# Sixteen gate and up column pairs as seven block products each, their weight sums built in DRAM by adding transfers

## What is computed

```
h2 = rmsnorm(x, norm2_g)
x = x + (silu(h2 @ w_ffn_gate) * (h2 @ w_ffn_up)) @ w_ffn_down
```

## Time and profile before

| | |
|---|---|
| median of 3 runs | 3119.81 us |
| span of the profiled execution | 3118.1 us |
| what lies around the span, against the median | 1.7 us |
| PE busy | 3085.6 us, 99% |
| DVE busy | 1740.3 us, 56% |
| ACT busy | 1082.3 us, 35% |
| POOL busy | 311.3 us, 10% |
| moved by transfers | 536.49 MB, 172 GB/s mean |
| transfer queues | hardware 52.8% of 16 engines |

### The profile page before, as it was taken

How to read it: one execution, slowest core, us unless ns; L and a number is a source line. 1 busy time by engine, 2 the same in 40 slices (tenths; PEclk the granted TensorE clock), 3 DMA queues, 4 the chain that set the end, 5 groups by cost and what they waited for, 6 DMA issues and landing times.

```text
span 3118.1 us, 66114 instructions
## 1 busy us (share of the span) xinstructions
PE 3085.6 (99%) x27707; PEld 2627.9 (84%) x27707; DVE 1740.3 (56%) x2975; ACT 1082.3 (35%) x1979; POOL 311.3 (10%) x285
## 2 busy tenths in 40 slices
PE   8999999999999999999999999999999999999998
PEld 6877878888888788888888888998888889999998
DVE  6565645457776768355566375304666535554444
ACT  5544433344444444332233243303333312321112
POOL 0011110001111100000111000001111100022220
PEclk9999999999999999999999999999999999999999
DMA  5476566337666675344444473265444455466664
GB/s 183 161 245 203 164 197 188 96 102 250 206 219 208 221 261 198 95 149 143 143 149 143 146 255 95 89 215 184 135 130 130 135 162 171 151 226 197 196 202 138
DMA packets 272694, 536.49 MB, mean 172 GB/s; under 512 B 36240, under 2 KB 39696, under 8 KB 272400
## 3 DMA queue, kind: packets, MB, share of 16 engines
q1 hardware_dynamic: 272400, 532.27, 52.8%
HBM read 420.17 MB, written 112.08 MB: 171 GB/s over the span
## 4 chain that ended last, share of the span: by engine, by line
PE 96%; DVE 1%; ACT 1%; DMA 1%; issue 1%; SPq 0%; DVEq 0%; ACTq 0%
PE PS L1045 81%; PE PS L1109 6%; PE PS L1063 3%; PE PS L1168 1%; PE PS L1234 1%; PE PS L1408 1%; PE PS L1218 1%; PE PS L1158 1%; PE PS L1415 0%; PE PS L1194 0%; PE PS L1204 0%; PE PS L1102 0%; PE PS L1103 0%; DMA raw<-w 0%; PE PS L1069 0%
## 5 line engine op out<-in xcount | busy, mean ns | idle before, releaser
L1045 PE MATMUL PS<-hh,wh 128*128 128x512 f32 x1864 | 749.3, 402 | 0.2
L1045 PE MATMUL PS<-hh,wl 128*128 128x512 f32 x1864 | 727.5, 390 | 0.0
L1045 PE MATMUL PS<-hl,wh 128*128 128x512 f32 x1864 | 726.9, 390 | 0.0
L1452 ACT ACTIVATE wh<-raw 128x512 fp32r<-128x512 f32 x452 | 283.7, 630 | 418.7 <-PE PS L1045 349.3
L1957 DVE TENSOR_TENSOR wl<-raw,wh 128x512 fp32r<-128x512 f32 x452 | 321.0, 713 | 182.7 <-ACT wh L1452 179.6
L1045 PEld LDWEIGHTS PS<-hh,wh 128*128 128x128 f32 x1864 | 349.8, 188 | 80.7 <-issue 3.0
L1045 PEld LDWEIGHTS PS<-hh,wl 128*128 128x128 f32 x1864 | 349.8, 188 | 75.6
L1045 PEld LDWEIGHTS PS<-hl,wh 128*128 128x128 f32 x1864 | 350.4, 188 | 68.5 <-issue 1.0
L1045 PE MATMUL PS<-fh,wh 128*128 128x512 f32 x528 | 213.3, 404 | 0.0
L1045 PE MATMUL PS<-hh_last,wh 128*128 128x272 f32 x1024 | 212.8, 289 | 0.1
L1045 PE MATMUL PS<-hl_last,wh 128*128 128x272 f32 x1024 | 211.4, 288 | 0.0
(11 more groups left out here) (370 smaller groups left out, 5270.9 us busy)
## 6 DMA issues: line engine op xcount, KB each, us to landing
wh<-weight_hi SPq DMA_DIRECT2D x480, 256.0 KB, 2.7
wl<-weight_lo SPq DMA_DIRECT2D x480, 256.0 KB, 3.1
raw<-w SPq DMA_DIRECT2D x192, 512.0 KB, 3.8
weight_hi<-wh SPq DMA_DIRECT2D x164, 256.0 KB, 4.4
weight_lo<-wl SPq DMA_DIRECT2D x164, 256.0 KB, 4.6
raw<-w SPq DMA_DIRECT2D x96, 256.0 KB, 3.0
xres<-x SPq DMA_DIRECT2D x48, 256.0 KB, 4.7
gate_scratch<-gst SPq DMA_DIRECT2D x48, 256.0 KB, 3.6
```

The lines of the kernel that those rows point to most:

```text
L1045: mm = pe.matmul(PS[:, bank(t) + f, 0:t.cols], wt[:, cols], mov[:, m, (t.half + f) * t.cols:(t.half + f + 1) * t.cols], start=(first and a ...
L1452: act.activation(wh[h % 4][:], src, ACT.Copy).then_inc(hi_done, 1)
```

## The change

All four pairs of each of the last four groups (16 pairs in place of 8) become product pairs, and `SEVENS` has 16 members. The weight sums are no longer made by POOL in SBUF. They are built for all 16 pairs in a DRAM tensor `weight_sums` in the two stretches of stages B and W of one block and A of the next (16 transfers from the start of stage B of block 0 on, 16 from that of block 1 on, 16 quanta apart), by transfers that POOL issues: for each group eight transfers of 1 MiB from DRAM to DRAM, four that write (the first of sums 0 and 3, the copies of sum 0 to sum 1 and of sum 1 to sum 2) and four that add what they read to what is there (`accum_op`). Step (u, (row, half)) takes gate (row 0) or up (row 1) and that half into sum u. SP then loads four finished sums of 256 KB for each product pair into `sf`. Since the transfers only add, some signs change: the gate and up results come out negated, and four DVE additions become subtractions, the tanh's scale and a scalar change sign.

```diff
-SEVENS = [j for s in range(2, len(GROUPS)) for j in (sum(GROUPS[:s]), sum(GROUPS[:s]) + 1)]
+FIRST7 = 2
+SEVENS = [j for s in range(FIRST7, len(GROUPS)) for j in range(sum(GROUPS[:s]), sum(GROUPS[:s + 1]))]
...
-                    if j == 0:
-                        self.seven(b, s, sum(GROUPS[:s]))
+                    if j % 2 == 0:
+                        self.seven(b, s, sum(GROUPS[:s]) + j)
...
+    summed = nc.dram_tensor("weight_sums", (128, 4, len(SEVENS), WP), F32, kind="Internal").ap()
...
         def sum_tag(j, u):
             n = SEVENS.index(j)
-            return plan.first_of(SEVENS[n - n % 2]) - (58.0, 28.0)[n % 2] + 5.0 * u
+            if n % 4 < 2:
+                return plan.first_of(SEVENS[n - n % 2]) - (58.0, 28.0)[n % 2] + 5.0 * u
+            return plan.first_of(SEVENS[n - 2]) + 13.0 + 4.5 * u
...
+        SUM_STEPS = ((0, (1, 0)), (3, (0, 0)), (0, (1, 1)), (3, (1, 0)), (1, 0), (1, (0, 0)), (2, 1), (2, (0, 1)))
+
+        def sums_tag(i):
+            b, i = divmod(i, 4 * len(SUM_GROUPS))
+            return Q["B", b] + 6.0 + 16.0 * i
...
-            def halves_raw():
-                for j in SEVENS:
...
-                        sp.dma_start(raw[i][:], w[u]).then_inc(s_ld[i], 16)
+            def sums_in():
+                for n, j in enumerate(SEVENS):
+                    for u in range(4):
+                        yield max(sum_tag(j, u) - 9.0, sum_tag(SEVENS[n - 1], u) + 5.0 if n else -100.0)
+                        if n == 0:
+                            sp.wait_ge(dense, Q["late", 0])
+                            sp.wait_ge(s_made[u], 16 * 2 * len(SUM_GROUPS))
+                        else:
+                            sp.wait_ge(s_lo, 4 * (n - 1) + u + 1)
+                        sp.dma_start(sf[u][:], summed[:, u, n, :]).then_inc(s_ld[u], 16)
...
-                        act.wait_ge(s_f, made_sum(j, u))
+                        act.wait_ge(s_ld[u], 16 * (n + 1))
...
             def weight_sums():
-                a11, a12, a21 = raw[0][:, 0:WP], raw[0][:, WP:WU], raw[1][:, 0:WP]
...
-                        pool.tensor_tensor(sf[u][:], one, two, op).then_inc(s_f, 1)
+                for i, (s, (u, source)) in enumerate(itertools.product(SUM_GROUPS, SUM_STEPS)):
+                    yield sums_tag(i)
+                    n0, g = SEVENS.index(sum(GROUPS[:s])), GROUPS[s]
+                    out = summed[:, u, n0:n0 + g, :]
+                    done = 2 * SUM_GROUPS.index(s)
+                    if i % 8 >= 2 or s != SUM_GROUPS[0]:
+                        pool.wait_ge(s_made[u], 16 * (done + sum(1 for v, _ in SUM_STEPS[:i % 8] if v == u)))
+                    if isinstance(source, int):
+                        pool.wait_ge(s_made[source], 16 * (done + 2))
+                        pool.dma_start(out, summed[:, source, n0:n0 + g, :]).then_inc(s_made[u], 16)
+                        continue
...
+                    if any(v == u for v, _ in SUM_STEPS[:i % 8]):
+                        pool.dma_start(out, part, accum_op=ALU.add).then_inc(s_made[u], 16)
+                    else:
+                        pool.dma_start(out, part).then_inc(s_made[u], 16)
...
-                dve.tensor_tensor(u2[:], p0[:], psv(p3), ALU.add).then_inc(evac["V"], 1)
+                dve.tensor_tensor(u2[:], p0[:], psv(p3), ALU.subtract).then_inc(evac["V"], 1)
```

More of the change, by code:

```diff
@@ L637, in hybrid_layer @@
         t_f, t_hi, t_lo = sem("t_sum"), sem("t_hi"), sem("t_lo")
-        s_ld = [sem(f"s_raw{i}") for i in range(2)]
-        s_f, s_hi, s_lo, p_v, p_r = sem("s_sum"), sem("s_hi"), sem("s_lo"), sem("p_sum"), sem("p_scaled")
+        s_ld = [sem(f"s_ld{u}") for u in range(4)]
+        s_made = [sem(f"s_made{u}") for u in range(4)]
+        s_hi, s_lo, p_v, p_r = sem("s_hi"), sem("s_lo"), sem("p_sum"), sem("p_scaled")
         stp_out, st_ld, s_out = sem("stp_out"), sem("st_ld"), sem("s_out")
@@ L736, in after @@
             return q0 + (at if at < 28 or q0 + 28 in plan.product else 28 + (at - 28) / 2)
+        SUM_GROUPS = list(range(FIRST7, len(GROUPS)))
+        SUM_STEPS = ((0, (1, 0)), (3, (0, 0)), (0, (1, 1)), (3, (1, 0)), (1, 0), (1, (0, 0)), (2, 1), (2, (0, 1)))
+        def sums_tag(i):
+            b, i = divmod(i, 4 * len(SUM_GROUPS))
+            return Q["B", b] + 6.0 + 16.0 * i
         def made_sum(j, u):
@@ L975, in small @@
                 sp.dma_start(st_s, st[:, :, 0:CH]).then_inc(s_out, 16)
-            run(small(), weights(), keep(), kept_again(), kept_aside(), halves_raw(), x_in(), x_res(), gates_out(), gates_in(), y_out())
+            run(small(), weights(), keep(), kept_again(), kept_aside(), sums_in(), x_in(), x_res(), gates_out(), gates_in(), y_out())
             sp.wait_ge(s_out, 16 * 6)
@@ L1547, in sevens @@
                     tanh_table()
-                    act.activation(e2[:, 0:MT], e1[:, 0:MT], ACT.Tanh, scale=0.5).then_inc(f_t, 1)
+                    act.activation(e2[:, 0:MT], e1[:, 0:MT], ACT.Tanh, scale=-0.5).then_inc(f_t, 1)
             def sevens_done():
@@ L1923, in weight_sums @@
             def weight_sums():
-                a11, a12, a21 = raw[0][:, 0:WP], raw[0][:, WP:WU], raw[1][:, 0:WP]
[L1925 to L1933, removed]
-                        pool.tensor_tensor(sf[u][:], one, two, op).then_inc(s_f, 1)
+                for i, (s, (u, source)) in enumerate(itertools.product(SUM_GROUPS, SUM_STEPS)):
[9 more added lines that the diff above has]
+                        continue
+                    row, half = source
+                    first = group_unit(s) + row
+                    part = w[first:first + 2 * g - 1:2, :, WP * half:WP * half + WP].rearrange("n p c -> p n c")
+                    if any(v == u for v, _ in SUM_STEPS[:i % 8]):
+                        pool.dma_start(out, part, accum_op=ALU.add).then_inc(s_made[u], 16)
+                    else:
+                        pool.dma_start(out, part).then_inc(s_made[u], 16)
             def scaled_sevens():
@@ L2159, in seven @@
                 dve.wait_ge(*freed(tile("P2", NB - 1, j)))
-                dve.tensor_tensor(e1[:, HT:MT], u2[:], p2[:], ALU.add).then_inc(p_v, 1)
+                dve.tensor_tensor(e1[:, HT:MT], u2[:], p2[:], ALU.subtract).then_inc(p_v, 1)
                 yield q0 + 20.1
@@ L2169, in seven @@
                 dve.wait_ge(*freed(p5))
-                dve.tensor_tensor(up[:, HT:MT], u3[:], p2[:], ALU.add).then_inc(p_v, 1)
+                dve.tensor_tensor(up[:, HT:MT], u3[:], p2[:], ALU.subtract).then_inc(p_v, 1)
                 yield q0 + 28.1
                 dve.wait_ge(dense, q0 + 28)
-                dve.tensor_tensor(up[:, 0:HT], u3[:], psv(p6), ALU.add).then_inc(evac["V"], 1)
+                dve.tensor_tensor(up[:, 0:HT], u3[:], psv(p6), ALU.subtract).then_inc(evac["V"], 1)
             def sevens_done():
@@ L2179, in sevens_done @@
                     dve.wait_ge(f_t, n + 1)
-                    dve.scalar_tensor_tensor(out=e1[:, 0:MT], in0=e2[:, 0:MT], scalar=1.0, in1=e1[:, 0:MT],
+                    dve.scalar_tensor_tensor(out=e1[:, 0:MT], in0=e2[:, 0:MT], scalar=-1.0, in1=e1[:, 0:MT],
                                              op0=ALU.add, op1=ALU.mult).then_inc(f_v, 1)
```

## The result

The changed kernel takes 3161.61 us (median of 4, 3158.17 to 3163.32) against 3119.41 us: slower by 1.3%, ratio 1.0132 with a 95% interval of 1.0121 to 1.0144. The forecast was 3113.7 us with a range of 3108 to 3123. The profiled execution has a span of 3159.7 us, 41.6 above the one before.

What follows compares the result with a forecast made beforehand. PE was taken to bound the kernel, busy 3085.6 of 3118.1 us. Terms -11.6 + 0.7 + 0 + 4.8 + 0 = -6.1 gave a span of 3112.0 and a median of 3113.7 us, range 3108 to 3123.

Steps and rivals of the forecast that it cites:

- -11.6: Last feed-forward: eight pairs change from 96 matmuls to 84, 1.45 us less each, 11.6 us less in all.
- stall term: Last feed-forward: PE stalls at P0 for late loads of sums, 1.2 us a group, four groups, +4.8 us.
- End of a group: `down` now follows a product pair; covered except in the last group, where Fd0's wait grows by 0.7 us.
- Pieces set aside: Their four loads (2 MiB) move to the very start of Fd0; price 0, bounds 0 and 2 us.
- The sums' loads: Last groups: sum 1, landing late, holds DVE's P5 read and PE's next P0; +4.8 us, bounds 0 and 13.
- The split between the pairs: P0 stalls in each of the last four groups: 0.3 us for the first pair, 0.9 for the second.
- The DRAM sums: 32 transfers issued by POOL in stages B, W and A: price 0, bounds nothing and 3 us.
- 32 transfers of 1 MiB, one in 48 matmuls.: Pace of the DRAM transfers in the two stretches: one each 10.9 us, from 732 matmuls in 166 us.
- stretches that now run at 119 and 149 GB/s, the transfer engines 0.39 and 0.45 busy: Load of the two stretches before the change, to which copies add 96 GB/s of reading and as much writing.
- the cover is the double buffer, one unit of eight quanta (5.5 us) and the ring behind it.: Weight loads beside the DRAM transfers: this cover set against raw loads that landed in 2.7 to 4.2 us.
- Rival (c): Adding transfers over some 16 us hold POOL, so `kk` of the next block starts late: 3123 us, chance 0.06.

Runs made afterwards that it cites:

- quiet_early: quiet with SP loading sum 1 together with sum 0, ahead of a ring piece: 3109.64 us against 3119.98 for the kernel before.
- late: Changed kernel, second set of 16 transfers started 60 quanta later in block 1's stage B, its first held until PE is there: 3117.15 us against 3120.45.
- nosums: Changed kernel without the 32 transfers; SP loads blocks of the weights in place of their sums: 3114.92 us against 3119.98 for the kernel before.
- quiet: Changed kernel, all 32 transfers held to PE's progress, second set from 66 quanta into block 1's stage B, 13 quanta apart: 3114.11 us against 3119.98.
- paced: Changed kernel, each of the 32 transfers held until PE has reached the quantum of its tag: 3122.85 us against 3120.45 for the kernel before.
- block2: Changed kernel, second set moved to the start of stage B of block 2, not held to PE: 3146.80 us, one run only.

## Why the prediction was wrong

**The last feed-forward, right in its mechanism and near in size.** The forecast for it was -11.6 + 0.7 + 0 + 4.8 = -6.1. Measured: -4.6 within the profile of the change, -5.1 in the run without transfers, -10.3 once the waits are gone. That last one tests the sum without its stall term: -11.6 + 0.7 = -10.9. Half a microsecond more went where the sum had no term: the wait for ACT's `e` near the end of the program grew from 1.9 to 2.4 us.

- *End of a group*: Fd0's wait went from 0.8 to 1.5 us, exactly the 0.7 said. No other group end shows a wait.
- *Pieces set aside*: 0, as said.
- *The sums' loads*: seven waits behind eight pairs, 3.8 us by the list and 4.9 us by PE's starts, against 4.8. The mechanism is the one described, and `quiet_early` removes the waits by moving that one load. A sum's load landed in a median of 4.8 us (I had taken 5.1), and DVE in order of time shows the P5 read (`u<-u,PS`) held behind the rest of sum 1, which waits for ACT:

```profile
3085.27 0.69 DVE L2215 TENSOR_TENSOR sl<-sf,sh 128x512 fp32r<-128x512 f32 x1 [2.04 <-ACT sh L1580]
3085.88 0.43 DVE L2185 TENSOR_TENSOR u<-u,PS 128x272 f32<-128x272 f32 x1
```

- PE in order of time at a P0 that had to wait:

```profile
2882.32 0.29 PE L1074 MATMUL PS<-tph,wl 128*128 128x272 f32 x1
2882.98 0.36 PE L1074 MATMUL PS<-hh_last,wh 128*128 128x272 f32 x1 [0.37 <-DVE u L2185]
```

- The split between the pairs, 0.3 for the first and 0.9 for the second, did not hold in any steady way. By the list the four groups show 0.4 and 0, 1.4 and 0.2, 0.3 and 0.7, 0.7 and 0.2; in the other runs now the one is longer and now the other. By starts their sum was 3.3 to 5.0 us in `late`, `nosums`, `quiet` and the changed kernel, so that it came out so near 4.8 is in part luck.
- By the rate of the Trainium skill (DMA: Bandwidth & Descriptors, § Bandwidth, 358 GB/s) there would have been no stall at all, by the prediction's estimate. The trace does not bear it out: there were seven waits behind eight pairs.

**The DRAM sums, wrong, and they decide the result.** I priced them at 0 with an upper bound of 3 us. They cost 45.3. Three steps of that paragraph failed.

1. *"32 transfers of 1 MiB, one in 48 matmuls."* A tag is a place in an engine's stream and no appointment. In `weight_sums` nothing waits for `dense`, the count of PE's finished work, so an idle POOL runs ahead and the transfers are paced by their own landing: 16 of them in 119 us (1134.6 to 1253.5), and before the stage starts. The working named the waits that the change adds, but did not ask which wait ties them to PE. Held to PE (`paced`), the kernel is 2.4 us above the one before, in place of 42.
2. *"stretches that now run at 119 and 149 GB/s, the transfer engines 0.39 and 0.45 busy"*. That is a mean over 166 us, and the second row begins at 1165. Cut finer, the kernel before shows this at the start of stage B in blocks 2, 0 and 1:

```profile
1826.00:1880.00 54.00, 53.57 (x233) 43.36 (x232) 48.65 (x77) 28.03 (x46) 0.00 (x0) 1.00 0.83 279
497.00:550.00 53.00, 53.00 (x236) 43.84 (x235) 34.38 (x52) 18.41 (x30) 0.00 (x0) 1.00 0.60 177
1161.00:1215.00 54.00, 53.56 (x231) 43.01 (x230) 48.35 (x77) 27.53 (x46) 0.00 (x0) 1.00 0.81 278
```

   Both blocks take their gates there; block 1 also writes its result, loads the input and residual and stores split weights, and stands at 0.81 where block 0 is at 0.60. The first set cost 2.9 us and the second 43.3. The difference between these two rows goes with that, and I had it in reach; `late` and `block2` bear it out.
3. *"the cover is the double buffer, one unit of eight quanta (5.5 us) and the ring behind it."* Weights were indeed what was late. But landing and cover were read from `raw` in block 0 and with the queue to itself, 2.7 to 4.2 us. With POOL's queue at work a unit of 512 KB landed in a median of 8.4 us and one raw load took 18.3 (issued at 1211.9), past the cover. ACT stood still for it, then DVE, and what PE waited for, `e` above all, was queued behind in their streams.

Rival (c) had the right cause, the transfers, at the wrong place: POOL's lateness for `kk`. It also asked for adds that take over 16 us; they took a median of 13.3. POOL was never late; its last transfer went out at 1253, well before. What suffered was the other queue. The price of 3123 that I gave it was also the end of the range. One more cost was in nobody's sum: among the waits part of the time was granted at PE's lower clock, 13.5 us on top of 29.9.

## What to carry to other kernels

Before moving traffic into an idle stretch, cut the stretch into pieces of some 20 us and read the share of the transfer engines in each; a mean over a stage says nothing about its first third. A transfer from an engine that is otherwise idle needs a wait on the pace-setting engine, or it runs as early and as densely as its own landings allow. Where a wait list names an operation that reads a late tile, look at what that operation's engine stood still for: here it was the weights ahead of `e`, and not the gates that `e` reads. In an in-order engine, look at what stands behind the operation that waits for a load: moving one load ahead of another was worth 4.5 us here.

## What the runs showed of the hardware

A second transfer queue that always had work took 52.9% of the engines' time and left the first 51.0%, where the first had used 82%; the loads of the gates landed in 12.6 us. Where the first queue had used 29.5% (1215 to 1310 us), the second took 67.1%, the first kept 27.1%, and PE lost nothing. Paced to 26%, at the crowded place, the second queue left 75.2%, and the gates landed in 6.2 us.

An adding transfer of 1 MiB from DRAM to DRAM lands in about twice the time of a plain one. In the kernel quiet, the adds and then the first writes:

```profile
DMA to landing us min/median/max: 9.1/10.1/12.4
```

```profile
DMA to landing us min/median/max: 5.0/5.3/7.4
```

Whether the sharing is strictly turn by turn, or follows what is in flight, was not tried. Nor was it whether it is the engines' time that runs short or the memory behind them.
